# Moving the last three of fifteen closing scan steps from VectorE to GpSimd, and one table load from GpSimd's queue to SyncE's

## What is computed

```
h = RMSNorm(x);  z = h @ W_in  -> q, k, v, u_ssm, gate_attn, gate_ssm
A = windowed attention(q, k, v)
B = bidirectional S5 scan of u_ssm (complex diagonal state), + D*u, GELU, GLU
merged = sigmoid(gate_attn) * (A @ W_ba) + sigmoid(gate_ssm) * (B @ W_bs)
x = x + RMSNorm(merged @ W_out)
x = x + RMSNorm(W_down(gelu(dwconv3(h2 W_gate)) * (h2 W_up)))
```

## Time and profile before

| what | value |
|---|---|
| median of 3 runs | 2648.36 us (2648.12 to 2657.18) |
| the profiled execution: its own time | 2653.53 us |
| the profiled execution: span of its instructions | 2651.7 us |
| mean granted clock of TensorE | 0.984 |
| busy share PE, DVE, ACT, POOL | 96%, 65%, 37%, 39% |
| DMA | 390.99 MB, mean 147 GB/s |

### The profile page before, as it was taken

How to read it: one execution, slowest core, us unless ns; L and a number is a source line. 1 busy time by engine, 2 the same in 40 slices (tenths; PEclk the granted TensorE clock), 3 DMA queues, 4 the chain that set the end, 5 groups by cost and what they waited for, 6 DMA issues and landing times. The chain is left out here.

```text
span 2651.7 us, 34579 instructions
## 1 busy us (share of the span) xinstructions
PE 2538.1 (96%) x12222; PEld 2084.9 (79%) x12222; DVE 1729.9 (65%) x2277; ACT 972.5 (37%) x1770; POOL 1025.8 (39%) x1187
## 2 busy tenths in 40 slices
PE   7999888999999899999989999999999999999898
PEld 6887777788887588888868888877888887788786
DVE  5211884687896175454687667788767777664886
ACT  5221777512211250123353333343333334532432
POOL 2072123387783000012244454334344434443542
PEclk9999999999999899999999999999999999999999
DMA  6483889644428736465434222213322223455465
GB/s 216 136 292 109 166 163 237 212 143 149 153 95 218 172 143 224 168 167 164 143 90 149 88 88 88 72 56 121 102 88 88 72 82 140 168 191 206 149 208 183
DMA packets 322597, 390.99 MB, mean 147 GB/s; under 512 B 52352, under 2 KB 255104, under 8 KB 314368
## 3 DMA queue, kind: packets, MB, share of 16 engines
q1 hardware_dynamic: 276224, 310.65, 39.2%
q10 hardware_dynamic: 40384, 46.72, 5.3%
q0 software_dynamic: 5824, 31.46, 3.4%
HBM read 255.07 MB, written 133.69 MB: 147 GB/s over the span
## 5 line engine op out<-in xcount | busy, mean ns | idle before, releaser
L529 PE MATMUL tl_banks<-gu_b_hi,gu_a_hi 128*128 128x512 f32 x1848 | 727.5, 394 | 33.2 <-DVE gu_b_lo L1984 19.4
L531 PE MATMUL tl_banks<-gu_b_lo,gu_a_hi 128*128 128x512 f32 x1848 | 724.6, 392 | 0.0
L530 PE MATMUL tl_banks<-gu_b_hi,gu_a_lo 128*128 128x512 f32 x1848 | 724.5, 392 | 0.0
L529 PEld LDWEIGHTS tl_banks<-gu_b_hi,gu_a_hi 128*128 128x128 f32 x1848 | 350.0, 189 | 116.4 <-issue 33.8
L531 PEld LDWEIGHTS tl_banks<-gu_b_lo,gu_a_hi 128*128 128x128 f32 x1848 | 350.3, 190 | 73.4
L530 PEld LDWEIGHTS tl_banks<-gu_b_hi,gu_a_lo 128*128 128x128 f32 x1848 | 350.5, 190 | 72.4
L1978 DVE TENSOR_TENSOR gu_a_lo<-gu_raw,gu_a_hi 128x512 fp32r<-128x512 f32 (+1 forms) x340 | 294.8, 868 | 146.6 <-ACT gu_a_hi L1675 146.5
L1675 ACT ACTIVATE gu_a_hi<-gu_raw 128x512 fp32r<-128x512 f32 (+1 forms) x340 | 208.7, 616 | 347.8 <-PE tl_banks L531 295.6
L1350 POOL TENSOR_TENSOR gu_s_one<-gu_raw 128x512 f32<-128x512 f32 (+1 forms) x68 | 91.7, 1348 | 347.6 <-DVE gu_a_lo L1978 210.2
L1363 POOL TENSOR_TENSOR gu_raw<-gu_s_one,gu_raw 128x512 f32<-128x512 f32 (+1 forms) x68 | 97.8, 1438 | 161.2 <-DVE gu_a_lo L1978 160.8
L148 PE MATMUL pi_banks<-pi_feat_hi,pi_w_hi 128*128 128x512 f32 (+1 forms) x344 | 131.2, 381 | 6.1 <-DVE pi_feat_lo L333 6.1
(11 more groups left out here) (315 smaller groups left out, 4974.6 us busy)
## 6 DMA issues: line engine op xcount, KB each, us to landing
gu_raw<-in_w_ffn_gate SPq DMA_DIRECT2D x44, 512.0 KB, 3.8
gu_raw<-in_w_ffn_up SPq DMA_DIRECT2D x44, 512.0 KB, 3.7
gs_w_raw<-in_w_in SPq DMA_DIRECT2D x40, 512.0 KB, 4.4
gates<-gs_gate_out ACTq DMA_DIRECT2D x64, 256.0 KB, 2.9
br_rows<-gates POOLq DMA_DIRECT2D x16, 1024.0 KB, 7.0
gu_raw<-f SPq DMA_DIRECT2D x32, 512.0 KB, 4.0
dn_y<-down_sums SPq DMA_DIRECT2D x16, 1024.0 KB, 5.0
down_sums<-dn_y SPq DMA_DIRECT2D x15, 1024.0 KB, 6.0
```

The source lines that it names most:

```text
L529: pe.matmul(out, w_hi, x_hi, start=first, stop=False, skip_group_check=again)
L530: pe.matmul(out, w_lo, x_hi, start=False, stop=False, skip_group_check=again)
L531: return pe.matmul(out, w_hi, x_lo, start=False, stop=last, skip_group_check=again)
```

## The change

POOL, when its own scan and its loads are issued, does the last three closing steps of DVE's scan (`run_tail`), into its own buffers `by_re` and `by_im`, counted by a new semaphore `tail`. It waits first for the end of its own scan and for the end of DVE's steps over the block ends; the closing steps each write one position of every block and read only the block ends, so that they don't depend on each other. DVE's list of steps ends after twelve closing steps, and `scan_pace` for slots 33, 34 and 35 becomes 5, 5 and 3. The load of the fourth outof table goes from POOL's queue to SP's, ahead of the local table. Readout and `u_last` wait for the semaphores that match.

```diff
--- before.py
+++ after.py
@@ -2441,6 +2441,7 @@
 POWERS = SSM_L + 1
 SCAN_I = 16
 SCAN_J = SSM_J // SCAN_I
+SCAN_TAIL = 3
 
 
 class SsmBases:
@@ -3269,7 +3270,7 @@
     N_WEIGHTS = len(weights)
 
 
-    scan_pace = [1] * 4 + [4] * 12 + [2] * 4 + [7] * 4 + [16] * 2 + [5] * 7 + [8, 8, 9] + [0] * 4
+    scan_pace = [1] * 4 + [4] * 12 + [2] * 4 + [7] * 4 + [16] * 2 + [5] * 7 + [5, 5, 3] + [0] * 4
     last_part = [max(n for n, part in enumerate(parts) if part[0] == w) for w in range(N_WEIGHTS)]
     first_part_of = [min(n for n, part in enumerate(parts) if part[2] == c) for c in range(CHUNKS)]
     last_part_of = [max(n for n, part in enumerate(parts) if part[2] == c) for c in range(CHUNKS)]
@@ -3320,6 +3321,7 @@
     y_ready = m.sem("y_ready")
     y_stored = [m.sem("y_stored0"), m.sem("y_stored1")]
     tables_in = m.pool_dma_sem("tables_in")
+    last_table_in = m.sem("last_table_in")
     local_in = m.sem("local_in")
     u_mid_in = m.pool_dma_sem("u_mid_in")
     u_last_in = m.pool_dma_sem("u_last_in")
@@ -3370,6 +3372,7 @@
                 load_features(3, range(2 * (w - 18), 2 * (w - 18) + 2))
 
         sync.wait_ge(gate_done, last_part_of[2] + 1)
+        sync.dma_start(outof_flat[3], outof_scratch[3]).then_inc(last_table_in, 16)
         for l in range(SSM_L):
             sync.dma_start(local_flat[l * SSM_CH:(l + 1) * SSM_CH].rearrange("p (a x) -> p a x", a=8),
                            local_scratch[l].rearrange("(a c) x -> c a x", a=8)).then_inc(local_in, 16)
@@ -3397,11 +3400,11 @@
         for l in range(SSM_L):
             pool.dma_start(u_mid[l * SSM_CH:(l + 1) * SSM_CH], u_chunks[l, :, first_mid:first_last]).then_inc(u_mid_in, 16)
 
-        pool.wait_ge(gate_done, last_part_of[2] + 1)
-        pool.dma_start(outof_flat[3], outof_scratch[3]).then_inc(tables_in, 16)
+        scans[0].run_tail(pool, scans[1])
 
         pool.wait_ge(scans[1].done, STEPS)
-        pool.wait_ge(scans[0].done, STEPS)
+        pool.wait_ge(scans[0].done, STEPS - scans[0].PER_STEP * SCAN_TAIL)
+        pool.wait_ge(scans[0].tail, scans[0].PER_STEP * SCAN_TAIL)
         for l in range(SSM_L):
             pool.dma_start(u_last[l * SSM_CH:(l + 1) * SSM_CH], u_chunks[l, :, first_last:]).then_inc(u_last_in, 16)
 
@@ -3446,8 +3449,10 @@
         pe.wait_ge(edge_zero, 2)
         for d in range(2):
             pe.wait_ge(into_copied[d], 2 * GROUPS)
-            pe.wait_ge(scans[d].done, STEPS)
-        pe.wait_ge(tables_in, 4 * 16)
+            pe.wait_ge(scans[d].done, STEPS - scans[d].PER_STEP * (0 if d else SCAN_TAIL))
+        pe.wait_ge(scans[0].tail, scans[0].PER_STEP * SCAN_TAIL)
+        pe.wait_ge(tables_in, 3 * 16)
+        pe.wait_ge(last_table_in, 16)
         pe.wait_ge(local_in, SSM_L * 16)
         for n in range(3):
             own_tokens(n)
@@ -3564,7 +3569,10 @@
 
     def add_semaphores(self, m):
         self.done = m.sem(f"scan_done{self.d}")
-        self.start = m.sem(f"scan_start{self.d}")
+        if self.on_pool:
+            self.start = m.sem(f"scan_start{self.d}")
+        else:
+            self.tail = m.sem(f"scan_tail{self.d}")
 
     def within(self, i):
 
@@ -3614,8 +3622,30 @@
             yield self.within(i)
         for i in range(SCAN_J - 1):
             yield self.of_last(i)
-        for i in range(SCAN_I - 1):
+        for i in range(SCAN_I - 1 - SCAN_TAIL):
             yield self.into_next(i)
+
+    def run_tail(self, engine, other):
+
+        tail, done = self.tail, 0
+        engine.wait_ge(other.done, self.PER_STEP * (2 * SCAN_I + SCAN_J - 3) + 1)
+        engine.wait_ge(self.done, self.PER_STEP * (SCAN_I + SCAN_J - 2) + 1)
+        for i in range(SCAN_I - 1 - SCAN_TAIL, SCAN_I - 1):
+            target, source, power, blocks, _ = self.into_next(i)
+            by_re, by_im = other.by_re[:, :, :, 0:blocks], other.by_im[:, :, :, 0:blocks]
+            for n, by in enumerate((by_re, by_im)):
+                factor = self.leaps[:, n, power, :].rearrange("p k (q b) -> p k q b", b=1)\
+                    .broadcast_to([P, 2, QS, blocks])
+                if done:
+                    engine.wait_ge(tail, done)
+                engine.tensor_tensor(by, source, factor, ALU.mult).then_inc(tail, 1)
+                done += 1
+            engine.wait_ge(tail, done)
+            engine.tensor_tensor(target, target, by_re, ALU.add).then_inc(tail, 1)
+            engine.wait_ge(tail, done + 1)
+            engine.tensor_tensor(target[:, 0:1], target[:, 0:1], by_im[:, 1:2], ALU.subtract).then_inc(tail, 1)
+            engine.tensor_tensor(target[:, 1:2], target[:, 1:2], by_im[:, 0:1], ALU.add).then_inc(tail, 1)
+            done += 3
 
     def over_blocks(self, engine):
         with engine.Fori(0, SCAN_J - 1) as i:
```

## The result

The changed kernel takes 2666.24 us (median of 7 runs, 2661.1 to 2672.11) where the kernel before, measured again beside it, takes 2652.66 us (7 runs, 2648.12 to 2658.89): a ratio of 1.0046, 95% interval 1.0033 to 1.0058, so 12.2 us slower (8.8 to 15.4). The prediction had the direction and the place, and about half of the size: +6.5 us. Of the 11.3 us between 2654.9 and 2666.24, 4.3 are that the kernel before has a median of 2652.66 with more runs instead of 2648.36.

The account below looks back on a forecast made before the run. PE, busy 96%, was taken to bound the kernel, with transfers setting the readout's start: 2.6 us later release plus 3.9 us table made +6.5 us, 2648.4 + 6.5 = 2654.9 us, range 2645 to 2660 us.

Parts of the forecast that it names:

- What bounds the stretch: Before the readout: its start, 855.94 in the old profile, is the number to forecast, set by the DMA transfers.
- the 866: Start of the readout on the old profile's time scale: later than 866 would show the prediction wrong; 862.4 was forecast.
- The tail's pace: POOL's tail beside DVE's scan: 8.13 us a DVE step, 8.92 us a POOL step, both ending at 839.0.
- Full exclusion: Rival in the tail: DVE and POOL exclude each other for whole instructions; +9.8 us, 2658.2 us, chance 0.06.
- The scans' end: End of DVE's scan: 839.0 instead of 839.57, about 0.6 us gained, u_last issued at about 839.6.
- The table: Fourth outof table on SP's queue ahead of the local transfers: costs 3.9 us, between 2.85 and 5 us.
- The rival of a hidden table: Rival at SP's queue: engines take the table in beside the local table's writes; about 2647.8 us, chance 0.22.
- SP's late release: SP's issues behind DVE's low half of slot 37 go out at 833.2 instead of 830.6: 2.6 us later.
- The sum: DMA chain of table, local table and u_last before the readout: 2.6 plus 3.9, +6.5 us; chance 0.60.
- What PE waits for: Before the readout: 8 to 10 us for a DMA instead of 2.4; 1 to 3 us before slot 37, another before 38.
- The clock's rival: Rival in the readout: PE's clock stays at half for long after idling some 9 us; 2666.9 us, chance 0.04.

Follow-up runs that it names:

- early_release: Changed kernel with DVE's last scan parts dealt out as 5, 2, 2, 4 instead of 5, 5, 3; ratio 1.0016 to the kernel before.
- pace_only: Kernel before with DVE's last scan parts dealt out as 8, 8, 5, 4 instead of 8, 8, 9; ratio 1.0009.
- table_only: Kernel before with the fourth outof table moved from POOL's queue to SP's, ahead of the local table, no tail; ratio 1.0010.
- tail_only: Changed kernel with the fourth outof table back on POOL's queue, between the first and second tail step; ratio 1.0029 to the kernel before.
- tail_early_release: Changed kernel with the table on POOL's queue between the first two tail steps and scan parts 5, 2, 2, 4; ratio 1.0005 to the kernel before.
- tail_later: Changed kernel with POOL's tail also waiting until DVE has ended its ninth closing step; ratio 1.0030 to the kernel before.
- rest_held: Changed kernel with the u_rest loads on SP's and ACT's queues held until the local table has landed; ratio 1.0039 to the kernel before.

## Why the prediction was wrong

**What bounds the stretch: right.** The start of the readout decided, and it was set by the transfers. The readout starts 61.67 us behind POOL's first load, which is 867.6 on the time scale of the profile before, past the 866 that the prediction had named as a sign of being wrong. That the transfers decide was shown from both sides: early_release has the latest scans and one of the small losses, and pace_only takes out the longest wait of PE and gains nothing.

**The tail's pace: right for DVE's step, too slow for POOL's.** I had 8.13 us for DVE's step and 8.92 for POOL's; measured were 7.69 and 8.03, and 7.7. Full exclusion, with 9.6 us for DVE's step, did not occur.

**The scans' end: right by luck.** The scans end 0.3 to 0.4 us earlier than before, where I had 0.6. Two errors cancel: the low half of slot 37 ends 3.4 us later than forecast, and DVE's three parts behind it take 3.0 us instead of 6.2, as POOL is through at 832.45 and not beside them.

**The table: right in size, to the tenth by luck.** 3.9 us was the middle of two bounds, taken for want of a row; 3.9 was measured by itself in table_only. It is no constant: from tail_only to the changed kernel the table costs 4.6 us, from tail_early_release to early_release 2.2. The rival of a hidden table is out in all three.

**SP's late release: the step that failed.** The sum had 2.6 us for it, with an upper bound of 4.8; it was 6.05. I counted DVE's slowed work from 812.17, as if the part ahead of it ran at the old pace. POOL begins its tail in the middle of that part, and there DVE lost 2.95 us, on two instructions of 240 elements, which tail_later gave back. The low halves held DVE 1.6 us longer than the 1.22 each that I took for the value; the steps themselves were 1.3 us quicker than forecast. 2.95 + 1.64 - 1.27 = 3.3 us, the difference between 2.6 and 6.05 but for 0.1. That low halves are stretched stood in the trace of the kernel before. Beside POOL's scan two of DVE's last three took about twice their 1.22 us:

```profile
790.42 2.23 DVE L3524 TENSOR_TENSOR gs_w_lo<-gs_w_raw,gs_w_hi 128x1024 fp32r<-128x1024 f32 x1
801.42 2.45 DVE L3524 TENSOR_TENSOR gs_w_lo<-gs_w_raw,gs_w_hi 128x1024 fp32r<-128x1024 f32 x1
```

**What the sum lacked.** 6.05 + 3.9 leaves 1.75 of the 11.7 us. About 1.4 of it is `u_rest`, whose loads start when the gates end and which in the changed kernel still meet the local table, as rest_held has it. I had counted the transfers ahead of the readout's data, and not those that would be started beside them once it is late. About 0.35 us is not accounted for. Since the parts are no constants, as the table's three prices show, this sum is a rough one. Beyond the stretch, the median that the forecast started from, 2648.4 us of 3 runs, was 4.3 us low; the right one would have brought the forecast to 2659.2 and left it below the measured time.

**What PE waits for: half right.** I expected the wait for `u_last`, 8 to 10 us of it. It was 13.2 us, for the local table: `u_last` shared the engines with it from 843 on and landed first, rather than behind it. Ahead of that I had a wait of about 1.3 us for the low half of slot 37 and another for that of slot 38; it was 4.8 us for slot 37, by the late low half, and none for slot 38.

**The clock: small.** PE idled for 13.2 us, the granted clock was still half (0.50) in the first 5 us of the readout, and its first twelve matmuls took 5.46 us instead of 4.31. In all it is 0.5 us from the readout's start to the end of the span, as the two profiles stand. The clock's rival had 2666.9 us, close to the 2666.24 measured, but by chance: it wanted 12 us from the clock.

Two windows of the profile after, between 858 and 870 us (us, busy PE, PEld, DVE, ACT, POOL, PEclk, DMA share, GB/s):

```profile
858.00:864.00 6.00, 0.00 (x0) 0.00 (x0) 0.00 (x0) 0.52 (x1) 0.00 (x0) 0.50 1.10 152
...
868.00:870.00 2.00, 2.00 (x6) 1.35 (x4) 0.00 (x0) 0.00 (x0) 0.00 (x0) 0.50 1.09 218
```

## What to carry to other kernels

When an engine is slowed by a neighbour, look for what in its order other queues wait for, and time that instruction, not the end of its work: here the scans ended as before, and one low half of weights in their midst, six microseconds late, held back a queue with 3 MB of loads. Count the slowed stretch from the neighbour's first instruction, inside whatever it falls into. And a wait of the busiest engine is worth only what is left when the next wait behind it is set against it: the 3.9 us here were worth nothing.

## What the runs showed of the hardware that I had not expected

Eight transfers of 256 KB into 16 partitions each keep the 16 DMA engines busy at 134 GB/s while nothing else moves, where a table of 1.18 MB into 128 partitions passes at 0.85 MB in 2 us, 424 GB/s. It makes no difference whether they come from one queue or from two (0.60 and 0.58 MB from 838 to 842 us). A load of 512 KB on SP's queue took 18.9 and 26.5 us to land beside them on POOL's, where it took 5.6 ahead of them in the kernel before. A VectorE instruction of 240 elements that takes 0.56 us alone took 2.58 us when GpSimd's first multiplications began beside it, which took 2.72 us together.
